# Diagonal taps on TensorE for a third of a long depthwise convolution, and GpSimd's products moved to VectorE

## The chip, the cores and the metric

The kernel runs on one core of one Trainium2 chip. A core has five engines that run side by side, each with an instruction queue of its own: TensorE (matrix products), VectorE, ScalarE and GpSimd (elementwise work), and SyncE, which here issues the weight loads. The engines wait for each other by counting semaphores. The metric is the device time of one execution, in microseconds (us); lower is better. The time before is 1533.48 us, the median of three runs (1533.14 to 1535.83).

## The reference, cut to what matters

Two transformer blocks run one after the other on 256 tokens of 1024 channels. The first one (attention and a feed-forward part) and the last part of the second (a feed-forward part with 16,384 experts) are not touched. The second block puts 16 meta tokens ahead and projects all 272 tokens to five parts: `z`, `xbc`, `dt` and the two halves `a` and `g` of a convolution branch. Two branches follow, and one output projection of both:

```python
def causal_depthwise_conv(x, w, b):          # every channel with its own taps
    y = lax.conv_general_dilated(x, w[:, None, :], window_strides=(1,), padding=[(k - 1, 0)],
                                 feature_group_count=x.shape[-1], ...)
    return y + b

def conformer_conv(u, conv_w, conv_b, ln_g, ln_b):      # conv_w: 31 taps x 1024 channels
    a, g = jnp.split(u, 2, axis=-1)
    h = causal_depthwise_conv(a * jax.nn.sigmoid(g), conv_w, conv_b)
    mu, var = mean(h), mean(square(h - mu))
    return jax.nn.silu((h - mu) * lax.rsqrt(var + EPS) * ln_g + ln_b)

def ssd_mixer(z, xbc, dt_raw, ...):
    xbc = jax.nn.silu(causal_depthwise_conv(xbc, conv_w, conv_b))    # 4 taps x 2048 channels
    xs, bm, cm = jnp.split(xbc, ...)
    dt = jax.nn.softplus(dt_raw + dt_bias)
    y = ssd_chunked(xs, dt, -exp(a_log), bm, cm)       # chunks of 128 tokens
    y = (y + d_skip * xs) * jax.nn.silu(z)
    return y * lax.rsqrt(mean over groups(y * y) + EPS) * norm_w
```

The long convolution is 31 taps on 1024 channels. With channels on the 128 partitions these are 8 channel tiles of 256 tokens, 8 x 31 = 248 products of a tile with one tap per channel.

## The kernel before, in words

**Weights.** All weights come as 423 units of 128x1024 float32. SyncE loads them into a ring of four (`raw`). ScalarE rounds a unit to its high half (`hi_to`, L825), VectorE subtracts to get the low half (`lo_to`, L1217), both into a ring of three (`W`). TensorE takes 24 matmuls per unit (L275 to L277): high by high, high by low, low by high. So a unit can be split only when the unit three before it is used up, and ScalarE's and VectorE's steps for later units stand in their queues between their other work. `hi_to(n)` and `lo_to(n)` mean "make all units below n".

**Order.** Every engine's program is written out by hand, with no scheduler. The part of the second block at issue runs so:

1. 16 GLU units (`U_GLU`). Even units give `g` (ScalarE's sigmoid, L1023), odd ones `a`; VectorE multiplies (L1391) into the tile `GP[j]`, which has 30 zero columns ahead of it. ScalarE makes the first of 31 products of a tile with the bias (`conv_first`, L1012).
2. 16 XB units (`U_XB`), 2048 channels of `xbc`. ScalarE copies them (L1030) and makes the first of the four short taps (L1034), VectorE the three others (L1406).
3. Eight z units (`U_Z`), between which stand: the `dt` product on TensorE (L549), softplus on ScalarE and VectorE (L1419 to L1425), the cumulative sums (L555 to L557), transposes of `xs` and `bm` (L568, L578), the products with `dt` (`XDT`, L1434), the state products (L595). After ScalarE's last short-convolution work come eight Silu (L1038).
4. The layer norm: TensorE adds up the eight tiles of `CV` over the channels (L604, waits for all 31 taps of each), VectorE subtracts the mean (L1453), ScalarE squares, TensorE sums again (L283), root, reciprocal, gains, Silu.
5. The core phase: eight steps `core_a(n)`, `core_b(n)` of the chunked scan with eight units of the output projection (`conformer_units`) between them.

**The long taps.** VectorE does the other 240 products (`long_convs`, L1379): `CV[j] = GP[j] shifted * tap + CV[j]`, two tiles by turns, 30 taps each. They are dealt out as filler: five after each GLU unit from the fifth on, four after each XB unit, 15 in each `z_step`, and the rest (26) behind the last `z_step`. Queues are in order, so what stands behind a group of fillers waits for them.

**GpSimd** does twelve products of this block: two 128x2048 products `DTU` (L1741), two 1024-wide `XDE` (L1748), and eight 128x512 products of `CM` (L1755) in the core phase.

## Time and profile before

| | us |
|---|---|
| median of three runs | 1533.48 |
| the profiled execution | 1532.85 |
| its span, first to last instruction | 1531.0 |
| TensorE busy | 1417.4 (93%) |
| VectorE busy | 1095.0 (72%) |
| ScalarE busy | 700.1 (46%) |
| GpSimd busy | 24.7 (2%) |
| L1379, the long taps, x240 | 101.4 |
| L1217, the low halves, x423 | 518.3 |

The page also cuts the span in 40 slices of 38.3 us and gives the busy share of each in tenths; granted clock 10 is full speed, 2.4 GHz.

```profile
PE   6999699998998548889999999999999999999997
...
DVE  4555466544899995665799997788879888655554
```

PE is TensorE, DVE VectorE, ACT ScalarE, POOL GpSimd. VectorE is at nine tenths or more in the slices 12 to 15, 421 to 574 us, and TensorE is at its lowest in two of these.

### The profile page before, as it was taken

The numbers are of one execution on the slowest core, as the hardware profiler recorded it, in microseconds if no ns is written. First come the engines' busy times: TensorE is split into PE (matmuls) and PEld (weight loads), VectorE is DVE, ScalarE is ACT, GpSimd is POOL, SyncE is SP. The second block draws the span as 40 slices with busy tenths as digits, with TensorE's granted clock in tenths as the row PEclk, the third lists the DMA queues.
The fourth block names the chain that finished last, engine by engine and source line by source line (L and its number), as shares of the span: only waits on it lengthen the run. The fifth ranks groups of instructions, "written<-read, shape, count | busy, mean of one in ns | idle before, by whom it ended". The sixth has DMA issues, their size and how long they took to land.

```text
span 1531.0 us, 25947 instructions
## 1 busy us (share of the span) xinstructions
PE 1417.4 (93%) x10882; PEld 1294.0 (85%) x10882; DVE 1095.0 (72%) x1773; ACT 700.1 (46%) x939; POOL 24.7 (2%) x20
## 2 busy tenths in 40 slices
PE   6999699998998548889999999999999999999997
PEld 5877599997988547789999999999998888888886
DVE  4555466544899995665799997788879888655554
ACT  4554355443554416545544445333343343444443
POOL 0000000000000201100000000000000000000000
PEclk9999799999999679989999999999999999999999
DMA  6433155664444212246566556555555555566663
GB/s 230 113 97 97 42 173 185 194 196 135 126 150 138 69 42 70 62 123 176 153 190 187 185 180 187 158 158 160 153 160 157 165 156 162 172 187 191 198 188 110
DMA packets 63621, 228.64 MB, mean 149 GB/s; under 512 B 7313, under 2 KB 8209, under 8 KB 63377
## 3 DMA queue, kind: packets, MB, share of 16 engines
q1 hardware_dynamic: 61776, 223.90, 48.7%
q10 hardware_dynamic: 1728, 3.09, 0.5%
q8 instruction: 86, 1.41, 0.4%
q14 instruction: 31, 0.25, 0.0%
HBM read 225.91 MB, written 1.05 MB: 148 GB/s over the span
## 4 chain that ended last, share of the span: by engine, by line
PE 79%; DVE 16%; ACT 3%; issue 1%; DMA 1%; ACTq 0%; DVEq 0%
PE ps L275 15%; PE ps L276 15%; PE ps L277 15%; PE ps L779 8%; PE ps L781 8%; PE ps L780 8%; DVE plain L1379 6%; DVE W L1217 4%; PE ps L748 3%; PE ps L283 2%; DVE plain L1406 1%; DVE RSI L1223 1%; DVE plain L1230 1%; ACT W L825 1%; PE ps L435 1%
## 5 line engine op out<-in xcount | busy, mean ns | idle before, releaser
L1217 DVE TENSOR_TENSOR W<-raw,W 128x1024 fp32r<-128x1024 f32 x423 | 518.3, 1230 | 263.9 <-ACT W L825 263.7
L825 ACT ACTIVATE W<-raw 128x1024 fp32r<-128x1024 f32 x423 | 446.3, 1057 | 390.5 <-PE ps L781 216.1
L275 PE MATMUL ps<-XH,W 128*128 128x256 f32 (+1 forms) x1784 | 513.1, 288 | 17.6 <-DVE W L1217 15.3
L276 PE MATMUL ps<-XL,W 128*128 128x256 f32 (+1 forms) x1784 | 508.8, 285 | 0.0
L277 PE MATMUL ps<-XH,W 128*128 128x256 f32 (+1 forms) x1784 | 505.8, 284 | 0.0
L275 PEld LDWEIGHTS ps<-XH,W 128*128 128x128 f32 x1784 | 339.9, 191 | 20.3 <-issue 17.2
L277 PEld LDWEIGHTS ps<-XH,W 128*128 128x128 f32 x1784 | 341.8, 192 | 0.0
L276 PEld LDWEIGHTS ps<-XL,W 128*128 128x128 f32 x1784 | 340.3, 191 | 0.1
L779 PE MATMUL ps<-W,HH 128*128 128x512 f32 x512 | 205.6, 402 | 0.8 <-ACT hid L1182 0.8
L781 PE MATMUL ps<-W,HL 128*128 128x512 f32 x512 | 202.9, 396 | 0.0
L780 PE MATMUL ps<-W,HH 128*128 128x512 f32 x512 | 202.9, 396 | 0.0
L781 PEld LDWEIGHTS ps<-W,HL 128*128 128x128 f32 x512 | 96.4, 188 | 23.4
L779 PEld LDWEIGHTS ps<-W,HH 128*128 128x128 f32 x512 | 96.4, 188 | 23.1 <-issue 1.0
L780 PEld LDWEIGHTS ps<-W,HH 128*128 128x128 f32 x512 | 96.6, 189 | 22.0
L1379 DVE SCALAR_TENSOR_TENSOR plain<-plain,vec 128x256 f32<-128x256 f32 x240 | 101.4, 496 | 0.0
L1182 ACT ACTIVATE hid<-ps 128x512 f32<-128x512 f32 x64 | 38.3, 599 | 118.8 <-PE ps L277 118.7
L276 PE MATMUL ps<-F1L,W 128*128 128x256 f32 x256 | 70.7, 276 | 0.0
L275 PE MATMUL ps<-F1H,W 128*128 128x256 f32 x256 | 70.7, 276 | 0.0
L277 PE MATMUL ps<-F1H,W 128*128 128x256 f32 x256 | 70.7, 276 | 0.0
L1648 DVE TENSOR_TENSOR onehot<-onehot,RSI 128x1536 bf16<-128x1536 bf16 x64 | 61.0, 953 | 0.0
L1644 DVE TENSOR_TENSOR onehot<-RSI 128x1024 bf16<-128x1024 bf16 x64 | 44.3, 692 | 22.2 <-PE ps L748 21.5
L748 PEld LDWEIGHTS ps<-onehot 128*128 128x128 bf16 x1536 | 50.0, 97 | 10.3 <-issue 8.8
(268 smaller groups left out, 1630.6 us busy)
## 6 DMA issues: line engine op xcount, KB each, us to landing
raw<-in_w_dn SPq DMA_DIRECT2D x128, 512.0 KB, 3.7
raw<-in_w_up SPq DMA_DIRECT2D x128, 512.0 KB, 3.6
raw<-in_w_ff SPq DMA_DIRECT2D x64, 512.0 KB, 4.1
raw<-in_w_in SPq DMA_DIRECT2D x57, 512.0 KB, 3.7
raw<-in_w_out SPq DMA_DIRECT2D x24, 512.0 KB, 3.7
raw<-in_w_q SPq DMA_DIRECT2D x16, 512.0 KB, 3.7
raw<-in_w_kv SPq DMA_DIRECT2D x4, 512.0 KB, 3.7
plain1a<-in_memT ACTq DMA_DIRECT2D x1, 1024.0 KB, 11.0
```

The source lines that it names most:

```text
L275: e.matmul(out, wh, xh, start=first, stop=False, skip_group_check=shared)
L276: e.matmul(out, wh, xl, start=False, stop=False, skip_group_check=shared)
L277: return e.matmul(out, wl, xh, start=False, stop=last, skip_group_check=shared)
L748: t = e.matmul(ps[b][:, r * 64:r * 64 + 64], OA[:, r // 2, :, r % 2], OB[:, r // 2, j, :, r % 2], start=j == 0, stop=j == 2)
L779: e.matmul(ps[b][:, :], HH[:, c % 8, tok], wh, start=c == 0, stop=False)
L780: e.matmul(ps[b][:, :], HH[:, c % 8, tok], wl, start=False, stop=False)
L781: return e.matmul(ps[b][:, :], HL[:, c % 8, tok], wh, start=False, stop=c == 127)
L825: e.activation(W[:, u % NSLOT, 0, :], raw[:, u % NRAW, :], ACT.Copy).then_inc(s["hi"], 1)
L1217: e.tensor_tensor(W[:, u % NSLOT, 1, :], raw[:, u % NRAW, :], W[:, u % NSLOT, 0, :], ALU.subtract).then_inc(s["lo"], 1)
L1379: e.scalar_tensor_tensor(CV[:, j, :], GP[:, j, 16 + k:272 + k], V("ccw", 31 * j + k), CV[:, j, :], ALU.mult, ALU.add).then_inc(cv[j], 1)
L1644: e.tensor_tensor(OA, pairs(IOTA, 128), at(0, 128), ALU.is_equal).then_inc(s["oa"], 1)
L1648: e.tensor_tensor(OB.rearrange("p t q a b -> p (t q) a b"), EB.rearrange("p (t q a) -> p t q a", t=4, q=1) .broadcast_to([128, 4, 3, 128]) ...
```

## The change

78 of the 248 products go to TensorE: taps 0 to 7 of the tiles 4 and 5, and all 31 of the tiles 6 and 7. For each, ScalarE writes a 128x128 matrix with the tap's 128 channel values on its diagonal (`diagonals`, the identity times a column), into a ring of 64 that lies where the output halves `YCH`, `YCL` will be written later. TensorE multiplies it with the shifted tile and adds up in PSUM bank 7 (tiles 4, 5) and 0 (tiles 6, 7). ScalarE copies the sum with the bias to `CV` (`conv_out`). VectorE keeps 166 products: tiles 0 to 3 from tap 1 on, 4 and 5 from tap 8 on. Its fillers are four per GLU unit, two per XB unit, 14 per `z_step`, two left at the end. The z units use PSUM banks 5 and 6 only. GpSimd's twelve products of this block are done by VectorE, each at a written place.

```diff
+CONV_AT = {3: (0, 1), 7: (2, 3)}
+PE_TAPS = [(j, k) for j, n in ((4, 8), (5, 8), (6, 31), (7, 31)) for k in range(n)]
+NDIAG = 64
...
-        z_bank = (5, 6, 7, 0)
+        z_bank = (5, 6, 5, 6)
...
+            def conv_taps():
+                for p, (j, k) in enumerate(PE_TAPS):
+                    if k == 0:
+                        e.wait_ge(s["xb"], 12 if j < 6 else 13)
+                        e.wait_ge(s["gp"], j + 1)
+                        e.wait_ge(s["pads"], 2)
+                    e.wait_ge(s["diag"], p + 1)
+                    e.matmul(ps[7 if j < 6 else 0][:, half(j)], DIAG[:, p % NDIAG, :], GP[:, j, 16 + k:272 + k],
+                             start=k == 0, stop=...).then_inc(s["cp"], 1)
+                    yield
...
             t.then_inc(s["dt_mm"], 1)
+            tap(8)
             next(z)
+            tap(8)
             e.wait_ge(s["dt_v"], 3)
...
             next(z)
+            tap(8)
...
+                    else:            # after the second transpose group of each chunk
+                        tap(8)
...
+            tap(8)
             next(z)
+            tap(len(PE_TAPS))
...
             def conformer_units():
-                e.wait_ge(s["z_out"], 4)
+                e.wait_ge(cv[6], 31)
+                e.wait_ge(cv[7], 31)
...
+            def diagonals():
+                e.wait_ge(s["unit"], U_GLU)
+                for p, (j, k) in enumerate(PE_TAPS):
+                    if p >= NDIAG:
+                        e.wait_ge(s["cp"], p - NDIAG + 1)
+                    e.activation(DIAG[:, p % NDIAG, :], ident, ACT.Copy,
+                                 scale=V("ccw", 31 * j + k)).then_inc(s["diag"], 1)
+                    yield
+            def conv_out(j, n):
+                e.wait_ge(s["cp"], max(p for p, (i, _) in enumerate(PE_TAPS) if i // 2 == j // 2) + 1)
+                e.activation(CV[:, j, :], ps[7 if j < 6 else 0][:, j % 2 * 256:j % 2 * 256 + 256], ACT.Identity,
+                             bias=V("ccb", j)).then_inc(cv[j], n)
...
+                for _ in range(2):   # once behind each of the 32 GLU and XB units
+                    next(diags)
...
             next(z)
+            conv_out(4, 8)
+            conv_out(5, 8)
+            for _ in diags:
+                pass
...
             next(z)
+            conv_out(6, 31)
+            conv_out(7, 31)
...
-                for tiles in ((0, 1), (2, 3), (4, 5), (6, 7)):
-                    for k in range(1, 31):
+                for tiles, first in (((0, 1), 1), ((2, 3), 1), ((4, 5), 8)):
+                    for k in range(first, 31):
...
-                    for _ in range(5):
+                    for _ in range(4):
...
-                for _ in range(4):
+                for _ in range(2):
...
-                for _ in range(15):
+                for _ in range(14):
```

The three kinds of GpSimd products (`DTU`, `XDE`, `CM`) are taken out of its program and put into VectorE's, with the same operands: `DTU` before the second `z_step`, `XDE` after each chunk's second `XDT`, `CM` right after each product of `LT` in the core phase.

VectorE between the `dt` step and the second chunk's transposed products. Before (L1379 the taps, L1422 and L1425 the `dt` step, L1217 the low halves, L1434 `XDT`):

```order
283 L1379 SCALAR_TENSOR_TENSOR plain<-plain,vec 128x256 x15
284 L1422 SCALAR_TENSOR_TENSOR small<-small 128x48
285 L1425 SCALAR_TENSOR_TENSOR small<-small 128x48
286 L1217 TENSOR_TENSOR W<-raw,W 128x1024
287 L1379 SCALAR_TENSOR_TENSOR plain<-plain,vec 128x256 x15
288 L1434 TENSOR_TENSOR plain<-ps,small 16x512
289 L1217 TENSOR_TENSOR W<-raw,W 128x1024
290 L1379 SCALAR_TENSOR_TENSOR plain<-plain,vec 128x256 x15
291 L1434 TENSOR_TENSOR plain<-ps,small 16x512
292 L1434 TENSOR_TENSOR plain<-ps,small 128x512
```

And of the changed kernel (L1446 the taps, L1489 and L1492 the `dt` step, L1284 the low halves, L1497 `DTU`, L1507 `XDT`, L1514 `XDE`):

```order
283 L1446 SCALAR_TENSOR_TENSOR plain<-plain,vec 128x256 x14
284 L1489 SCALAR_TENSOR_TENSOR small<-small 128x48
285 L1492 SCALAR_TENSOR_TENSOR small<-small 128x48
286 L1284 TENSOR_TENSOR W<-raw,W 128x1024
287 L1497 TENSOR_TENSOR plain<-cstb,small 128x2048 x2
288 L1446 SCALAR_TENSOR_TENSOR plain<-plain,vec 128x256 x14
289 L1507 TENSOR_TENSOR plain<-ps,small 16x512
290 L1284 TENSOR_TENSOR W<-raw,W 128x1024
291 L1446 SCALAR_TENSOR_TENSOR plain<-plain,vec 128x256 x14
292 L1507 TENSOR_TENSOR plain<-ps,small 16x512
293 L1514 TENSOR_TENSOR plain<-plain,small 16x1024
294 L1507 TENSOR_TENSOR plain<-ps,small 128x512
```

The two `DTU` products stand ahead of 14 taps, and the `XDE` product of the first chunk ahead of the second chunk's first `XDT`.

TensorE at the end of the stretch. Before, from the last state products (L595) on, the two z matmuls that follow standing for a whole unit:

```order
3203 L568 MATMUL ps<-cst,plain 128x128 x4
3204 L595 MATMUL ps<-plain 128x256 x8
3205 L275 MATMUL ps<-XH,W 128x256
3206 L276 MATMUL ps<-XL,W 128x256
...
3228 L277 MATMUL ps<-XH,W 128x256
3229 L604 MATMUL ps<-plain,cst 128x256 x8
```

And of the changed kernel (L564 the taps, L629 the state products, L640 the channel sums):

```order
3208 L600 MATMUL ps<-cst,plain 128x128 x4
3209 L564 MATMUL ps<-plain,diag 128x256 x8
3210 L629 MATMUL ps<-plain 128x256 x8
3211 L564 MATMUL ps<-plain,diag 128x256 x8
3212 L283 MATMUL ps<-XH,W 128x256
3213 L284 MATMUL ps<-XL,W 128x256
...
3236 L564 MATMUL ps<-plain,diag 128x256 x22
3237 L640 MATMUL ps<-plain,cst 128x256 x8
```

Eight taps stand on either side of the state products, and 22 directly ahead of the channel sums.

## Rows read from the trace of the kernel before

**Rows 1.** busy time by stage, with (instructions); granted clock, DMA share, GB/s

```profile
core 0: us, PE busy (x) PEld busy (x) DVE busy (x) ACT busy (x) POOL busy (x), PEclk, DMA share, GB/s
403.00:440.00 37.00, 36.78 (x293) 36.50 (x292) 37.00 (x75) 16.04 (x23) 0.00 (x0) 1.00 0.53 157
440.00:480.00 40.00, 33.11 (x257) 32.16 (x256) 40.00 (x82) 21.45 (x34) 0.00 (x0) 1.00 0.48 144
513.00:574.00 61.00, 30.83 (x185) 27.86 (x185) 56.99 (x116) 12.87 (x18) 11.50 (x4) 0.72 0.15 43
595.00:652.00 57.00, 51.48 (x382) 39.87 (x380) 37.77 (x56) 30.48 (x46) 10.28 (x8) 1.00 0.26 75
```

**Rows 2.** VectorE in order of time: start, us, instruction, [idle before <-releaser]

```profile
441.44 1.23 DVE L1217 TENSOR_TENSOR W<-raw,W 128x1024 fp32r<-128x1024 f32 x1
...
504.75 0.22 DVE L1419 TENSOR_TENSOR small<-ps,vec 128x48 f32<-128x48 f32 x1
...
506.08 6.02 DVE L1379 SCALAR_TENSOR_TENSOR plain<-plain,vec 128x256 f32<-128x256 f32 x15
...
512.26 0.21 DVE L1425 SCALAR_TENSOR_TENSOR small<-small 128x48 f32<-128x48 f32 x1
514.99 2.25 DVE L1217 TENSOR_TENSOR W<-raw,W 128x1024 fp32r<-128x1024 f32 x1 [2.52 <-ACT W L825]
517.16 9.38 DVE L1379 SCALAR_TENSOR_TENSOR plain<-plain,vec 128x256 f32<-128x256 f32 x15
...
557.69 16.31 DVE L1379 SCALAR_TENSOR_TENSOR plain<-plain,vec 128x256 f32<-128x256 f32 x41
575.78 2.74 DVE L1453 SCALAR_TENSOR_TENSOR plain<-ps,plain 128x256 f32<-128x256 f32 x8 [1.77 <-PE ps L604]
```

**Rows 3.** the chain that ended last, in order of time: start, us, what

```profile
573.66 2.08 PE ps L604 x4
579.21 3.47 PE ps L283 x16
```

**Rows 4.** VectorE by line and shape, whole span: busy us, mean ns, idle before

```profile
L1586 DVE TENSOR_TENSOR hid<-hid,cst 128x2048 f32<-128x2048 f32 x4 | 9.0, 2285 | 0.0
```

**Rows 5.** GpSimd in order of time, columns as in group 2

```profile
512.54 8.16 POOL L1741 TENSOR_TENSOR plain<-cstb,small 128x2048 f32<-128x2048 f32 x2 [145.08 <-DVE small L1425]
...
544.47 1.90 POOL L1748 TENSOR_TENSOR plain<-plain,small 128x1024 f32<-128x1024 f32 x1 [7.71 <-DVE plain L1434]
```

**Rows 6.** ScalarE in order of time, columns as in group 2

```profile
499.45 4.51 ACT L1038 ACTIVATE plain<-plain 128x544 f32<-128x544 f32 x8
503.87 1.04 ACT L825 ACTIVATE W<-raw 128x1024 fp32r<-128x1024 f32 x1
...
509.76 0.22 ACT L1058 ACTIVATE small<-vec 128x16 f32<-128x16 f32 x1
```

**Rows 7.** ScalarE by line and shape, 380 to 600 us

```profile
L1012 ACT ACTIVATE plain<-plain,vec 128x256 f32<-128x256 f32 x8 | 4.8, 596 | 12.6 <-DVE plain L1391 12.6
```

**Rows 8.** TensorE in order of time, columns as in group 2

```profile
436.23 0.36 PE L275 MATMUL ps<-XH,W 128*128 128x272 f32 x1 [0.22 <-DVE W L1217]
...
496.38 5.43 PE L549 MATMUL ps<-WDT,plain 128*128 128x16 f32 x48
```

**Rows 9.** TensorE by line and shape, 512 to 575 us

```profile
L568 PE MATMUL ps<-cst,plain 128*128 128x128 f32 x16 | 3.0, 316 | 9.8 <-DVE plain L1434 9.8
L595 PE MATMUL ps<-plain 128*128 128x256 f32 x8 | 2.0, 392 | 0.0
```

**Rows 10.** VectorE in the core phase, columns as in group 2

```profile
618.01 0.69 DVE L1472 TENSOR_TENSOR plain<-plain,ps 128x512 f32<-128x512 f32 x1 [1.22 <-ACT plain L1097]
619.44 1.46 DVE L1217 TENSOR_TENSOR W<-raw,W 128x1024 fp32r<-128x1024 f32 x1 [0.74 <-ACT W L825]
```

**Rows 11.** two short stretches, columns as in group 1

```profile
528.00:536.00 8.00, 1.35 (x7) 1.15 (x7) 6.80 (x17) 1.53 (x2) 1.12 (x1) 0.50 0.25 66
544.00:552.00 8.00, 7.55 (x49) 6.69 (x49) 7.25 (x15) 2.14 (x3) 1.90 (x1) 1.00 0.19 66
```

More of the change, by code:

```diff
@@ L149, in build @@
             (8, 272), (8, 272), (8, 272), (8, 302), (8, 256), (16, 275), (16, 272), (8, 256), (8, 256), (2, 272)])
-        YCH, YCL = (tensor(P2, n, [128, 16, 256], F32R) for n in ("YCH", "YCL"))
+        P2a = stack()
+        YCH, YCL = (tensor(P2a, n, [128, 16, 256], F32R) for n in ("YCH", "YCL"))
+        P2a.close()
+        P2b = stack()
+        DIAG = tensor(P2b, "diag", [128, NDIAG, 128])
+        P2b.close()
         DTU = [plain2[:, at:at + 2048].rearrange("p (a b) -> p a b", b=128) for at in (8 * 272, 16 * 272)]
@@ L539, in z_units, with tap @@
                 for m in range(8):
-                    if m % 2 == 0:
-                        e.wait_ge(s["xb"], (10, 11, 12, 13)[m // 2])
+                    if m < 4:
+                        if m % 2 == 0:
+                            e.wait_ge(s["xb"], 10 + m // 2)
+                    elif m % 2 == 0:
+                        e.wait_ge(s["z_out"], m // 2 - 1)
                     h_unit(U_Z + m, ps[z_bank[m // 2]][:, half(m)], slice(16, 272))
                     yield
+            def conv_taps():
[6 more added lines that the diff above has]
+                    e.matmul(ps[7 if j < 6 else 0][:, half(j)], DIAG[:, p % NDIAG, :], GP[:, j, 16 + k:272 + k],
+                             start=k == 0, stop=p + 1 == len(PE_TAPS) or PE_TAPS[p + 1][0] != j).then_inc(s["cp"], 1)
+                    yield
+            taps = conv_taps()
+            def tap(n):
+                for _ in range(n):
+                    next(taps, None)
             z = z_units()
@@ L659, in core_b @@
                     e.wait_ge(s["st_v"], 4)
+                    e.wait_ge(cv[4], 8)
+                    e.wait_ge(cv[5], 8)
                 for r in range(4):
@@ L1013, in conv_first @@
                              scale=V("ccw", 31 * j)).then_inc(cv[j], 1)
+            def diagonals():
[6 more added lines that the diff above has]
+                    yield
+            diags = diagonals()
+            def conv_out(j, n):
+                e.wait_ge(s["cp"], max(p for p, (i, _) in enumerate(PE_TAPS) if i // 2 == j // 2) + 1)
+                e.activation(CV[:, j, :], ps[7 if j < 6 else 0][:, j % 2 * 256:j % 2 * 256 + 256], ACT.Identity,
+                             bias=V("ccb", j)).then_inc(cv[j], n)
             for m in range(16):
@@ L1035, in scalar_program @@
                                      scale=V("scw", 4 * i)).then_inc(s["xi"], 1)
+                for _ in range(2):
+                    next(diags)
             for i in range(0, 16, 2):
@@ L1407, in vector_program @@
                                                    ALU.mult, ALU.add).then_inc(s["xc"], 1)
-                for _ in range(4):
+                for _ in range(2):
                     next(convs, None)
@@ L1426, in vector_program @@
                                    ALU.mult).then_inc(s["dt_v"], 1)
+            lo_to(U_Z + 1 + 3)
+            e.wait_ge(s["dt_v"], 3)
+            for c in range(2):
+                e.tensor_tensor(DTU[c], upper.rearrange("p (a b) -> p a b", a=1).broadcast_to([128, 16, 128]),
+                                DTA[:, 1 + c, :].rearrange("p (a b) -> p a b", b=1)
+                                .broadcast_to([128, 16, 128]), ALU.mult).then_inc(s["du"], 1)
             z_step(1)
@@ L1437, in vector_program @@
                         z_step(2 + c)
+                if c < 2:
+                    e.wait_ge(s["xdt"], 2 * c + 2)
+                    e.wait_ge(s["dc_a"], 2)
+                    e.tensor_tensor(per_head(XDE[c][0:n, :]), per_head(XDT[c][0:n, :]),
+                                    spread(DC[0:n, c * 16:c * 16 + 16], n, 16), ALU.mult).then_inc(s["xde"], 1)
             for hf in range(2):
@@ L1474, in vector_program @@
                                     ALU.mult).then_inc(s["ltm"], 1)
+                    g, c = divmod(n, 2)
+                    e.wait_ge(s["cm"], n + 1)
+                    e.tensor_tensor(q4(CM[:, n % 2, :]), q4(CM[:, n % 2, :]),
+                                    XO[:, 12 + g, 16 + 128 * c:144 + 128 * c].rearrange("p (a b) -> p a b", a=1)
+                                    .broadcast_to([128, 4, 128]), ALU.mult).then_inc(s["cmm"], 1)
                 if n in (0, 1, 2, 4, 5, 6, 8, 9):
@@ L1737, in gpsimd_program @@
             e.memset(XB[:, :, 0:3], 0.0).then_inc(s["pads"], 1)
-            e.wait_ge(s["dt_v"], 3)
-            e.wait_ge(s["dt_mm"], 1)
-            for c in range(2):
-                e.tensor_tensor(DTU[c], upper.rearrange("p (a b) -> p a b", a=1).broadcast_to([128, 16, 128]),
-                                DTA[:, 1 + c, :].rearrange("p (a b) -> p a b", b=1)
-                                .broadcast_to([128, 16, 128]), ALU.mult).then_inc(s["du"], 1)
-            for c in range(2):
-                n = chunk[c][1]
-                e.wait_ge(s["xdt"], 2 * c + 2)
-                e.wait_ge(s["dc_a"], 2)
-                e.tensor_tensor(per_head(XDE[c][0:n, :]), per_head(XDT[c][0:n, :]),
-                                spread(DC[0:n, c * 16:c * 16 + 16], n, 16), ALU.mult).then_inc(s["xde"], 1)
-            for n in range(8):
-                g, c = divmod(n, 2)
-                e.wait_ge(s["cm"], n + 1)
-                e.tensor_tensor(q4(CM[:, n % 2, :]), q4(CM[:, n % 2, :]),
-                                XO[:, 12 + g, 16 + 128 * c:144 + 128 * c].rearrange("p (a b) -> p a b", a=1)
-                                .broadcast_to([128, 4, 128]), ALU.mult).then_inc(s["cmm"], 1)
         block = ctx.enter_context(nc.Block())
```

3 lines of the change are left out of this document (1 added, 2 removed).

## The prediction

> **What bounds the kernel now.** I read the stages first: how busy each engine is between two times. Up to 440 us TensorE and VectorE are both full. From 440 to 574 us VectorE alone is full, 40.0 of 40.0 and 57.0 of 61.0 us, while TensorE falls to half busy and to a mean granted clock of 0.72 [rows 1]. Then VectorE in order of time: its tap products L1379 run back to back, and behind the sixth weight split stand 41 of them in one block, up to 573.9 us; the mean subtraction L1453 starts at 575.78 [rows 2]. The chain that ended last runs through that block, then through the last two channel sums of L604 [rows 3]. So the end of this stretch is VectorE's number of products. The 51.5 busy us of 57 on TensorE in the core phase [rows 1] say that this phase belongs to TensorE.
>
> **What goes from VectorE, and what comes.** A product costs 6.02/15, less the overlap of one, so 0.396 us [rows 2]. VectorE loses 14 products of tiles 4 and 5 and 60 of tiles 6 and 7: 74 x 0.396 = 29.3 us. It gains two 128x2048 products before the channel sums; the same shape in another stage takes 2.285 us [rows 4], 2.2 paced, so 4.4 us. And two 1024-wide ones at the price of a weight split, 1.14 (506.08 less 504.75, less 0.19 for L1419) [rows 2], 2.3 us. Part of that was already paid: GpSimd's 8.16 us [rows 5] lie over a split of 2.25 us and 15 products of 9.38 us, where 1.14 and 5.94 are usual [rows 2]: 4.5 us lost by VectorE. So moving these two costs nothing net, and VectorE's own balance is -29.3 - 0.1 + 2.3 = about -27 us.
>
> The Trainium skill says in "SBUF — State Buffer", section "Who interferes with whom", that GpSimd and a VectorE operation with two SBUF inputs take an exclusive lock on a shared port pair, for whole instructions. The rows above agree as to direction; by a full exclusion the old place would have cost 8.2 us and not 4.5, the move would gain 3.7 us more, and since the second XDT (below) hangs on it, the time would be 1519.8.
>
> **What comes onto TensorE.** 78 products of a 128x128 float32 diagonal with 256 float32 columns. The shape stands in L283: 16 records are 8 products in 3.47 us, 0.434 each, at full clock; at half clock L604 shows 2.08 us for two [rows 3]. 78 x 0.434 = 33.9 us. I take that; the other end is 78 x 1.04 = 81 us. **Onto ScalarE** come 78 diagonals of 128x128 with a scale column, less four first taps. Between 0.22 us (128x16) [rows 6] and 0.60 us (128x256 with a column each of scale and bias) [rows 7]; I take 0.35, so 27 us, of which 64 lie in the two projection loops, where a pair of units leaves ScalarE 2 us free and more.
>
> **Walking it through.** "Unit" is a weight unit: 24 matmuls, 37.0/293 x 24 = 3.0 us on TensorE [rows 1].
> - GLU units: both engines were full [rows 1]. VectorE loses two products, 0.8 us, per pair of units, and falls below TensorE's 6.0. TensorE ran at its own pace already, so it ends about where it did, 436.0 us, 0.2 before the first XB unit [rows 8].
> - XB units: VectorE's pair is (504.75 - 441.44)/8 = 7.91 [rows 2], now less four products, 6.33; TensorE 6.0. The first pair waits some 1.5 us for ScalarE's first-tap operation, then VectorE is 0.3 us per pair slower than TensorE. The 16 units took 496.38 - 436.23 = 60.2 us [rows 8] and now 49.5: TensorE is through at 485.5, VectorE at 491 instead of 504.7.
> - Hand-over, with less cover than before. ScalarE has to finish eight Silu (4.5 us) before it makes the high half of the third z unit; that one ended at 504.9 [rows 6], 8.5 us behind the last XB unit (496.4 [rows 8]). With two diagonals more: 485.5 + 8.5 + 0.7 = 494.7. VectorE waits there for some 3.5 us; it did not wait before. Behind that wait stand its tap products and the step L1425, at 501.9 instead of 512.3 (split 1.14, 14 products 5.5, two small ones). Then ScalarE's next high half, which stands behind the sums of TensorE, lets VectorE wait: 2.5 us in the trace [rows 2], now 3.6, since TensorE first finishes eight of its taps. The next split ends at 506.6, the two 2048-wide products at 511.0, 14 products at 516.5, the first XDT at 517.2, split and 14 products more, the second XDT at 524.5.
> - TensorE meanwhile: dt product 5.1 us (with half clock behind it, as its 5.43 us of 16-column matmuls do no dense work [rows 8]), 8 taps, a unit, 8 taps, the cumulative sums from 502.9, a unit, 8 taps, a unit, 8 taps; at 518.3 it waits for the second XDT until 524.5. From there on it has its own work to do: five groups of transposes (0.6 each), three units (9.0), 46 taps (20.0), four state products (4.0) [rows 9], eight channel sums (3.5): 39.5 us, and 2.1 us for one unit at half clock behind the 6 us idle. That is 566.1.
> - VectorE has its last product done at 555.7. So **TensorE becomes the bound**: the block of 22 taps behind the last-but-two z unit, then two ScalarE copies that lie beside the first six channel sums.
> - The channel sums ended at 575.74 and end at 566.1: 9.6 us. Behind them the norm is the same chain; the next z unit runs at full clock instead of partly at half, 0.3 us. ScalarE's load of the root table, which lay beside the 41 products, now follows the two copies directly, up to 0.6 us against.
> - Core phase: VectorE takes eight 128x512 products of 0.6 us. They go into the waits for ScalarE's split, 0.74 us behind an L1472 of 0.69 [rows 10], and TensorE does not wait for them. Zero, within 1 us either way. If the cover fails, 8 x 0.6 = 4.9 us. Everything later is untouched.
>
> Sum: 9.6 + 0.3 = 9.9 us, call it 10. The profiled execution took 1532.85 us for a span of 1531.0; that gives 1522.9. The median of the runs is 0.6 us above it, so **1523.5 us**. With the cheap ends (diagonals 0.22, no half clock behind the wait) it is 13 us less than before, with the dear ones (diagonals 0.60, each hand-over 1 us later, half clock on some eight taps and a unit more) 4 us less: 1520 to 1529.
>
> **Rivals.**
> - *TensorE stays at 1.2 GHz through the taps: slower.* The clock is at 0.50 in the stretch 528 to 536 us, where TensorE worked 1.35 us of 8, and it stays at 0.72 on the mean of the whole stage; against it, 544 to 552 us, with transposes and float32 products in it, has 1.00 at 7.55 busy us of 8 [rows 1, 11]. If the 35.5 us of matmuls behind the second XDT all ran at half clock the sums would end near 600, 24 us later than now: 1557.8. It turns slower than before from 9.7 us of additional half-clock work on, a fourth of what lies there. The Trainium skill, "TensorE: Matmul & The Clock Gate", section "Loop structure matters more than you think", warns that long waits between groups of matmuls make them run cold; I expect one such wait of 6 us, for the second XDT, where the stage had several.
> - *The taps are hidden, VectorE still bounds.* If TensorE does not wait for XDT, or its taps cost 0.25 us, the end is VectorE's, 555.7 plus 2 for the last sums: 18 us gained, 1515.5. For it: TensorE was idle for half of 513 to 574 us [rows 1]. Against: L283's 0.434.
> - *The hand-overs eat it.* Four engines now pass diagonals, taps, XDT and halves round in strict order. There are eight places in which VectorE waits for a transpose or a high half that now stands behind eight taps (3.5 us) or diagonals. At 0.8 us each over what I have, 6.4 us are lost and 3.5 gained: 1530.0. For it: VectorE waited only 2.5 us for ScalarE with more cover [rows 2]. Against: most of these waits are on an engine that isn't the bound.
> - *The change doesn't take the products away* is excluded: the order of VectorE shows 166 where 240 were.
>
> **Chances and range.** A measurement of this kernel tells 0.2%, 3 us, from no change. Forecast 0.68; TensorE cold 0.08; hidden taps 0.10; hand-overs 0.14, half of it within 0.2%. So faster 0.86, same 0.06, slower 0.08. The range takes the forecast's own ends, and reaches toward both rivals of the same sign: 1515 to 1531.
>
> **What will show it.** VectorE's last tap product near 556 and TensorE's last channel sum near 566, with a block of 22 taps right before; if VectorE's is the later, the second rival. A tap pair of records at 0.43 us; at 0.87 or more the first. Granted clock of 485 to 566 us above 0.85. An idle stretch of TensorE of about 6 us before the transposes of the second chunk. L1425's successor at 501.9. GpSimd empty after its memsets. From the mean subtraction on, all times shifted by one amount; if the core phase is longer or shorter by over 1 us, that step is wrong.

## The result, and the profile after

The changed kernel takes **1525.8 us** (median of five runs, 1521.76 to 1526.07); the kernel before, beside it on the same chip, 1533.49 (five runs, 1533.14 to 1535.83). The ratio is 0.994, with a 95% interval of 0.9926 to 0.9955. The forecast was 1523.5, with a range of 1515 to 1531. The profiled execution of after took 1521.76 us for a span of 1520.0, and is the fastest of the five by 3.5 us; the one of before took 1532.85.

Busy time of after by stage, in the columns of [rows 1]; the last row is the short stretch behind TensorE's wait for the second `XDT`:

```profile
403.00:440.00 37.00, 37.00 (x297) 37.00 (x297) 34.17 (x66) 24.55 (x48) 0.00 (x0) 1.00 0.59 172
440.00:480.00 40.00, 39.43 (x308) 38.48 (x307) 37.74 (x72) 30.40 (x62) 0.00 (x0) 1.00 0.55 160
480.00:513.00 33.00, 32.91 (x223) 30.47 (x222) 26.66 (x49) 26.20 (x51) 0.00 (x0) 0.95 0.36 110
513.00:574.00 61.00, 54.66 (x312) 49.37 (x311) 46.08 (x99) 15.41 (x27) 0.00 (x0) 0.94 0.14 43
524.00:532.00 8.00, 5.40 (x26) 5.41 (x27) 7.97 (x16) 0.00 (x0) 0.00 (x0) 0.57 0.10 34
```

TensorE is full where VectorE was [rows 1], and its mean clock from 513 to 574 us is 0.94 where it was 0.72. Instead of VectorE's idle-free row there is a VectorE that waits. In order of time, columns as in group 2 (L1284 the low halves, L1446 the taps, L1492 the end of the `dt` step, L1497 `DTU`, L1507 `XDT`, L1531 the mean subtraction):

```profile
497.69 1.23 DVE L1284 TENSOR_TENSOR W<-raw,W 128x1024 fp32r<-128x1024 f32 x1 [3.44 <-ACT W L864]
...
504.61 0.21 DVE L1492 SCALAR_TENSOR_TENSOR small<-small 128x48 f32<-128x48 f32 x1
507.50 1.23 DVE L1284 TENSOR_TENSOR W<-raw,W 128x1024 fp32r<-128x1024 f32 x1 [2.69 <-ACT W L864]
508.65 4.49 DVE L1497 TENSOR_TENSOR plain<-cstb,small 128x2048 f32<-128x2048 f32 x2
513.05 5.63 DVE L1446 SCALAR_TENSOR_TENSOR plain<-plain,vec 128x256 f32<-128x256 f32 x14
...
525.87 0.67 DVE L1507 TENSOR_TENSOR plain<-ps,small 16x512 f32<-16x512 f32 x1
...
550.84 6.42 DVE L1446 SCALAR_TENSOR_TENSOR plain<-plain,vec 128x256 f32<-128x256 f32 x16
567.10 2.74 DVE L1531 SCALAR_TENSOR_TENSOR plain<-ps,plain 128x256 f32<-128x256 f32 x8 [9.85 <-PE ps L640]
```

The 41 products ahead of the mean subtraction [rows 2] are 16, and VectorE then waits 9.85 us for TensorE. TensorE in the same stretch (L578 the `dt` product, L564 the new taps, L600 transposes of `xs`, L640 the channel sums):

```profile
488.58 5.43 PE L578 MATMUL ps<-WDT,plain 128*128 128x16 f32 x48
493.86 5.39 PE L564 MATMUL ps<-plain,diag 128*128 128x256 f32 x16
501.93 3.62 PE L564 MATMUL ps<-plain,diag 128*128 128x256 f32 x16
...
526.60 1.12 PE L600 MATMUL ps<-cst,plain 128*128 128x128 f32 x4 [6.34 <-DVE plain L1507]
...
553.94 9.67 PE L564 MATMUL ps<-plain,diag 128*128 128x256 f32 x44
563.44 3.62 PE L640 MATMUL ps<-plain,cst 128*128 128x256 f32 x16
```

16 records are eight taps. At full clock they take 3.62 us; those behind the `dt` product, partly at half clock, 5.39. On the whole page the chain that ended last has moved the same way (before it was PE 79%, DVE 16%):

```profile
PE 88%; DVE 7%; ACT 3%; issue 1%; DMA 1%; ACTq 0%; DVEq 0%
```

### How the runs are compared

Kernels of this study differ by a few us, and executions of one kernel differ by as much. So the tables use a length inside the profile, too: the **stage** from VectorE's reciprocal of the norm ahead of the projection to the reciprocal of the long convolution's norm. Of after, these two are at 384.49 and at

```profile
573.90 1.75 DVE L1290 RECIPROCAL RSI<-RSI 128x256 f32<-128x256 f32 x1 [2.93 <-ACT RSI L877]
```

and of before at 381.88 and 583.21. The stage took 201.33 us and takes 189.41, so it is 11.9 us shorter.

Two half-clock stretches stand in nearly every such stage, one some 4 us behind its start and one behind the `dt` product. Each lasts 3.4 or 6.8 us, and this varies between executions of the same kernel. "Short" below means that both last 3.4 us, "long" that both last 6.8. A third one, behind TensorE's wait for the second `XDT`, is not counted in these words: it comes and goes with that wait (6.8 us in both profiles of after, 3.4 with `DTU` back on GpSimd, none with the early `XDT`).

### The profile page after: what moved, and what is told of

It reads as the page before. It is cut to its first block, busy times and chain, and to the rows that moved or that the text cites. A ratio compares the mean times of both kernels' runs of the same rounds, so it can differ in the third digit from the quotient of the medians.

```text
span 1520.0 us, 26271 instructions
## 1 busy us (share of the span) xinstructions
PE 1444.5 (95%) x11038; PEld 1317.7 (87%) x11038; DVE 1070.7 (70%) x1711; ACT 722.5 (48%) x1017; POOL 2.5 (0%) x8
## 4 chain that ended last, share of the span: by engine, by line
PE 88%; DVE 7%; ACT 3%; issue 1%; DMA 1%; ACTq 0%; DVEq 0%
PE ps L283 17%; PE ps L284 17%; PE ps L285 17%; PE ps L818 8%; PE ps L820 8%; PE ps L819 8%; PE ps L787 3%; PE ps L564 2%; PE ps L291 2%; DVE W L1284 2%; DVE RSI L1290 1%; DVE plain L1297 1%; DVE plain L1446 1%; ACT W L864 1%; PE ps L443 1%
## 5 line engine op out<-in xcount | busy, mean ns | idle before, releaser
L1284 DVE TENSOR_TENSOR W<-raw,W 128x1024 fp32r<-128x1024 f32 x423 | 514.8, 1222 | 266.7 <-ACT W L864 266.1
L283 PE MATMUL ps<-XH,W 128*128 128x256 f32 (+1 forms) x1784 | 509.8, 286 | 9.3 <-DVE W L1284 5.2
L283 PEld LDWEIGHTS ps<-XH,W 128*128 128x128 f32 x1784 | 336.7, 189 | 11.5 <-issue 7.0
L283 PE MATMUL ps<-F1H,W 128*128 128x256 f32 x256 | 70.7, 276 | 0.0
L1446 DVE SCALAR_TENSOR_TENSOR plain<-plain,vec 128x256 f32<-128x256 f32 x166 | 68.5, 475 | 0.0
```

Of the source, the lines that this page charges most:

```text
L283: e.matmul(out, wh, xh, start=first, stop=False, skip_group_check=shared)
L1284: e.tensor_tensor(W[:, u % NSLOT, 1, :], raw[:, u % NRAW, :], W[:, u % NSLOT, 0, :], ALU.subtract).then_inc(s["lo"], 1)
L1446: e.scalar_tensor_tensor(CV[:, j, :], GP[:, j, 16 + k:272 + k], V("ccw", 31 * j + k), CV[:, j, :], ALU.mult, ALU.add).then_inc(cv[j], 1)
```

## The experiments

Each label ran beside the kernel before; ratios are given with their 95% interval. The stage and its clock are those of the one profiled execution.

| kernel | median us (runs) | ratio | stage, us | clock |
|---|---|---|---|---|
| before | 1533.49 (5) | | 201.33 | short |
| after | 1525.8 (5) | 0.994 [0.9926, 0.9955] | 189.41 | short |
| after again | 1522.79 (6) | 0.992 [0.9908, 0.9932] | 193.03 | long |
| GpSimd back | 1521.51 (4) | 0.9915 [0.9899, 0.9932] | 190.43 | long |
| only GpSimd's products moved | 1535.4 (10) | 1.0 [0.9986, 1.0014] | 204.05 | long |
| 70 taps | 1521.33 (4) | 0.9915 [0.9883, 0.9947] | 189.64 | long |
| high half early | 1523.82 (4) | 0.9937 [0.9922, 0.9953] | 189.41 | short |
| 22 products omitted | 1516.23 (4) | 0.9878 [0.9864, 0.9893] | 184.90 | long |
| taps between `dt` groups | 1521.37 (5) | 0.9915 [0.9903, 0.9928] | 189.69 | first long, second gone |
| `DTU` back | 1521.72 (4) | 0.991 [0.9889, 0.9932] | 190.39 | long |
| early `XDT` | 1514.74 (4) | 0.9887 [0.9859, 0.9914] | 183.01 | short |
| early `XDT` again | 1516.63 (4) | 0.9875 [0.986, 0.9891] | 186.45 | long |
| early, mixed, `DTU` back | 1516.01 (6) | 0.9879 [0.9859, 0.9899] | 182.86 | first short, second gone |
| combined | 1516.37 (4) | 0.9876 [0.9856, 0.9897] | 187.57 | first long, second gone |

### How far runs of one kernel differ: after again

No edit.

> The changed kernel once more, unchanged, beside the others on one chip. Its five runs lay at 1521.8 once and at 1525.2 to 1526.1 four times, and the profiled one was the 1521.8. Theory A (the runs differ by how long TensorE stays at half clock behind its idle or thin stretches, here behind the dt product: 3.4 us in the profiled run, 6.8 us in two other kernels with the same code there, 1.7 us of delay each): runs at two or more levels some 2 to 4 us apart, median 1521 to 1526, and a trace with a longer or shorter half-clock stretch between 500 and 512 us. Theory B (drift of the chip): one level, shifted with the kernel before.

The stage is 3.62 us longer than in the first profile, with the same instructions. The windows 384:396 and 486:500 us, first of after and then of this run, columns as in group 1:

```profile
384.00:396.00 12.00, 7.67 (x46) 7.06 (x47) 9.37 (x16) 7.72 (x16) 0.00 (x0) 0.86 0.08 16
486.00:500.00 14.00, 14.00 (x94) 13.07 (x94) 10.39 (x21) 12.81 (x23) 0.00 (x0) 0.88 0.41 114
```

```profile
384.00:396.00 12.00, 9.76 (x49) 8.96 (x50) 8.94 (x17) 7.94 (x16) 0.00 (x0) 0.72 0.15 45
486.00:500.00 14.00, 14.00 (x82) 12.87 (x81) 10.38 (x21) 12.82 (x22) 0.00 (x0) 0.76 0.35 110
```

Twice the clock is low for 3.4 us more: 0.86 against 0.72 of 12 us, 0.88 against 0.76 of 14 us. In the second of these windows TensorE is never idle, and does 82 matmuls where it did 94. The second pair of profiles (early `XDT`, below) differs in the same two places, by 186.45 - 183.01 = 3.44 us: 1.7 us for each. From here on a stage is compared with one of the same clock. The runs lie between 1520.9 and 1526.0 us here and between 1521.8 and 1526.1 in the first set. Theory A fits that spread, but that each run's time is set by the length of these stretches is not shown, since only one run of each set has a profile.

### What gave the 11.9 us: GpSimd's products moved alone

The kernel before with its twelve GpSimd products at the places that they have after the change, and no tap on TensorE.

```diff
+            lo_to(U_Z + 1 + 3)
+            e.wait_ge(s["dt_v"], 3)
+            for c in range(2):
+                e.tensor_tensor(DTU[c], ...)         # VectorE, as after
...
-            for c in range(2):
-                e.tensor_tensor(DTU[c], ...)         # GpSimd
```

> The kernel before with only GpSimd's twelve products moved to VectorE at the places of the changed kernel; all 240 taps stay on VectorE, which bounds the stretch. Theory A: DTU net 0, XDE +2.3 less 0.5 of contention gone, so 1 to 2 us slower than before, 1535; core phase unchanged within 0.5 us. Theory B (full lock): 1.5 to 2 us faster than before. The core phase, if CM has no cover there, +4.9 us.

The ratio is 1.0, within 0.14% or 2.1 us either way, and both theories of the expectation (1 to 2 us slower, 1.5 to 2 us faster) lie within that. The trace is sharper. VectorE's last `dt` step and its mean subtraction, the rows of [rows 2] at 512.26 and 575.78, are here

```profile
514.80 0.21 DVE L1425 SCALAR_TENSOR_TENSOR small<-small 128x48 f32<-128x48 f32 x1
578.23 2.74 DVE L1464 SCALAR_TENSOR_TENSOR plain<-ps,plain 128x256 f32<-128x256 f32 x8 [1.77 <-PE ps L604]
```

`DTU` and `XDE` lie between the two, and the distance is 63.43 us where it was 63.52: nothing gained, nothing lost. The whole stage is 204.05 for 201.33, because of the clock at its two ends. Ahead of the `dt` step it is 1.8 us longer, with a first stretch of 6.8 us instead of 3.4. Behind the start of the mean subtraction it is 1.0 us longer, where TensorE's clock stays low for 3.5 us instead of 1.3. The stretch behind the `dt` product costs nothing in either kernel: behind it TensorE waits for VectorE, 6.25 us before and 4.67 here:

```profile
512.52 0.23 PE L555 MATMUL ps<-small,cstb 16*16 16x16 f32 x2 [6.25 <-DVE small L1425]
```

```profile
515.06 0.23 PE L555 MATMUL ps<-small,cstb 16*16 16x16 f32 x2 [4.67 <-DVE small L1425]
```

VectorE's eight `CM` products leave the core phase, from the reciprocal of the norm to the last group's, at 65.07 us, where it was 65.31.

So the gain is the taps', and the moved products have no part in it. This is also the only profile with all 240 taps on VectorE and a long clock; against after again, 193.03, it is 11.0 us longer, near the 11.9 between the two short ones.

### The taps' price: 70 instead of 78, and 22 left out

```diff
-((4, 8), (5, 8), (6, 31), (7, 31))
+((4, 4), (5, 4), (6, 31), (7, 31))      # VectorE takes the other eight
```

> The changed kernel with four instead of eight taps of the tiles 4 and 5 on TensorE (70 in all, 178 products on VectorE, whose last block is 10). Theory A (TensorE bounds the end of the stretch, VectorE was done 9.9 us before the mean subtraction): TensorE loses 8 x 0.434 = 3.5 us, VectorE gets 3.2 us more and is still earlier: 3.5 us faster than the changed kernel. Theory B (the hand-overs set it, not the amount of taps): same as the changed kernel. Theory C (VectorE bounds): 3.2 us slower.

```diff
-((4, 8), (5, 8), (6, 31), (7, 31))
+((4, 8), (5, 8), (6, 20), (7, 20))      # nobody does the other 22
```

> The changed kernel with 20 instead of 31 taps each of the tiles 6 and 7: 22 products are left out, nobody does them, so its output is another. It shows what TensorE's last block costs by itself. Theory A (TensorE bounds the end): the block of 22, 9.5 us, goes, VectorE (done 9.9 us before the mean subtraction) becomes the bound, the stretch ends 9 us earlier: 9 us faster than the changed kernel, VectorE's wait before the mean subtraction falls from 9.9 to 1 us. Theory B (amount of taps does not matter): the same time.

Against after again (193.03, same clock), eight taps less are worth 3.39 us, though VectorE has eight products more: 8 x 0.434 = 3.47. TensorE's taps are on the path, VectorE's are not. 22 taps less are worth 8.13 where they take 9.5. The end of the second shows why:

```profile
552.06 6.42 DVE L1446 SCALAR_TENSOR_TENSOR plain<-plain,vec 128x256 f32<-128x256 f32 x16
560.17 2.74 DVE L1531 SCALAR_TENSOR_TENSOR plain<-ps,plain 128x256 f32<-128x256 f32 x8 [1.69 <-PE ps L640]
```

The wait of 9.85 us is down to 1.69, about the 1.77 of [rows 2], where VectorE's own last product was what the sums waited for. VectorE has become the bound again, and it cuts the last 1.4 us. In both runs TensorE as the bound, theory A, is what came.

### The wait for the Silu: high half early

ScalarE makes the high half of the third z unit before its eight Silu instead of behind them.

```diff
+            hi_to(U_Z + 3)
             for i in range(0, 16, 2):
                 e.wait_ge(s["xc"], 3 * i + 6)
```

> The changed kernel with ScalarE's high half of the third z unit made ahead of the eight Silu instead of behind them. Theory A (VectorE waits 3.4 us for that half, but what comes next waits for TensorE's cumulative sums, which stand behind 16 taps and a unit): VectorE's wait of 3.4 us goes and reappears as a longer wait before the next split (2.7 plus 3.4 less 1); the kernel gains 0 to 1 us. Theory B (the wait is on the path): 3.4 us faster than the changed kernel.

The stage is 189.41, as in after to the hundredth. The wait of 3.44 us is gone, and its time stands further down the same queue:

```profile
502.56 0.21 DVE L1493 SCALAR_TENSOR_TENSOR small<-small 128x48 f32<-128x48 f32 x1 [1.39 <-ACT small L1120]
507.44 1.23 DVE L1285 TENSOR_TENSOR W<-raw,W 128x1024 fp32r<-128x1024 f32 x1 [4.67 <-ACT W L864]
```

The split that was at 507.50 is at 507.44. It waits for ScalarE's next high half, which stands behind TensorE's cumulative sums, and these stand behind a unit and 16 taps. So the visible wait was not on the path, as theory A had it.

### The price of the move to VectorE: GpSimd back, and DTU alone

```diff
-            for c in range(2):
-                e.tensor_tensor(DTU[c], ...)         # VectorE: DTU; and XDE, CM
...
+            for c in range(2):
+                e.tensor_tensor(DTU[c], ...)         # GpSimd, as before the change
```

> The changed kernel with GpSimd's twelve products (two 128x2048 DTU, two XDE, eight CM) given back to GpSimd; the taps stay on TensorE. Theory A (mine: the move costs VectorE nothing net, as GpSimd's 8.2 us of DTU cost VectorE 4.5 us in the old place, and CM is hidden): within 1 us of the changed kernel; the second XDT 1 us earlier at most, and the 14 taps beside DTU stretched by 4 to 5 us. Theory B (full exclusive lock): the time of both DTU, 8.2 us, is lost by VectorE before the second XDT, TensorE waits 3.7 us longer there, and the kernel is 3.7 us slower than the changed one. Theory C (the move is where part of the cost of the change lies): 2 to 5 us faster than the changed one.

The same with `DTU` alone:

> The changed kernel with only the two 128x2048 DTU products given back to GpSimd; XDE and CM stay on VectorE. From the traces of the GpSimd-back kernel (split of 4.00 us instead of 1.22 plus 4.49 of DTU) I expect the two products to cost VectorE 2.8 us on GpSimd and 4.4 on itself, since GpSimd starts them while VectorE waits for ScalarE's high half: second XDT 1.6 us earlier, kernel 1.6 us faster than the changed one at equal clock, of the 2.6 us that all twelve gave; from the split before DTU to the second XDT 16.7 us instead of 18.4. If the gain of all twelve came from XDE instead, this kernel is within 0.5 us of the changed one.

Stages 190.43 and 190.39, against 193.03: both save 2.6 us, so it is `DTU` that counts, and `XDE` and `CM` are worth nothing either way. Theory A of the first expectation, within 1 us of the changed kernel, fell, and C held; the second expected 1.6 us, and the second `XDT` came that much earlier. `DTU` alone, VectorE and then GpSimd:

```profile
509.99 3.99 DVE L1284 TENSOR_TENSOR W<-raw,W 128x1024 fp32r<-128x1024 f32 x1 [4.36 <-ACT W L864]
513.90 5.62 DVE L1446 SCALAR_TENSOR_TENSOR plain<-plain,vec 128x256 f32<-128x256 f32 x14
```

```profile
505.71 7.18 POOL L1818 TENSOR_TENSOR plain<-cstb,small 128x2048 f32<-128x2048 f32 x2 [137.23 <-DVE small L1492]
```

GpSimd works from 505.71 to 512.89, and VectorE waits until 509.99. So 2.9 us lie over VectorE's work, which is a split of 3.99 us (3.91 to its successor) instead of 1.15: 2.8 us lost, 4.4 saved, 1.6 net. The other 1.0 us comes behind it: TensorE waits 4.70 us for the second `XDT` instead of 6.36, and the half-clock stretch that follows lasts 3.4 us instead of 6.8.

### The wait for the second XDT: early XDT

Seven instead of 14 products in the z steps 1 and 2, so that VectorE reaches the first chunk's `XDT` earlier; the last block has 30 instead of 16.

```diff
-                for _ in range(14):
+                for _ in range((14, 7, 7, 14, 14, 14)[m]):
```

> The changed kernel with 7 instead of 14 filler taps in the second and third z steps of VectorE, the 14 taken out done at its end. Nothing is left out. Theory A (TensorE waits 6.3 us for the second XDT, and runs one unit at half clock behind it, on the path that sets the end): the second XDT comes 5.5 us earlier, the wait shrinks to about 1 us, the half-clock stretch goes, TensorE's last channel sum 6 to 8 us earlier, kernel 6 to 8 us faster than the changed one; VectorE's last tap stays near 557 and leaves 1 to 3 us of wait. Theory B (the wait is absorbed further on): same as the changed kernel.

> The changed kernel with seven instead of 14 products in the z steps 1 and 2, once more, beside the kernel that also takes the 128x2048 products back. Theory (half-clock stretches differ between executions of one kernel, and nothing else does): the stage is 183.0 us where the clock is low for 3.4 us three times between the norms, as in its first profile, and 1.7 us longer for each such stretch of 6.8 us; median 1513.5 to 1518 us. Rival (the first profile was a lucky one): stage above 187 us with the same clock.

The stage is 183.01 against 189.41 (both short), and 186.45 against 193.03 (both long): 6.4 and 6.6 us, in two pairs of profiles. In order of time on TensorE and by stage, of the first run:

```profile
518.84 0.66 PE L600 MATMUL ps<-cst,plain 128*128 128x128 f32 x4 [0.79 <-DVE plain L1507]
527.96 0.65 PE L600 MATMUL ps<-cst,plain 128*128 128x128 f32 x4 [1.28 <-DVE plain L1507]
...
513.00:566.00 53.00, 50.92 (x299) 45.40 (x298) 44.25 (x93) 13.81 (x21) 0.00 (x0) 1.00 0.16 50
```

The wait of 6.34 us is 0.79 and 1.28, and the clock behind it is 1.00. The medians are 1514.74 and 1516.63, against 1525.8 and 1522.79 for after. After was not run beside it, so the ratios to the kernel before are what can be compared: the second, up to 0.9891, lies clear of both of after's (from 0.9908 on), the first, up to 0.9914, touches one of them. The rival, that the first profile was a lucky one, falls with the second: 183.01 and two times 1.7 us are 186.4, and it was 186.45.

### The clock behind the dt product: taps between its groups

```diff
                                  stop=k == 7)
+                if i < 2:
+                    tap(4)
             t.then_inc(s["dt_mm"], 1)
             tap(8)
```

> The changed kernel with four of the first eight taps between the first and second, and four between the second and third group of the 16-column dt matmuls, which otherwise run 5.4 us in a row. Same work. Theory A (the half clock behind the dt product comes from that thin stretch): no half-clock stretch between 500 and 512 us, TensorE reaches the cumulative sums 2 to 3 us earlier, runs closer together, 1 to 3 us faster than the changed kernel in the median. Theory B (the clock falls there for another reason): the stretch stays, and dt is 3.5 us later with nothing gained.

The half-clock stretch is gone: TensorE's window from 488 to 513 us

```profile
488.00:513.00 25.00, 25.00 (x168) 23.16 (x167) 16.91 (x33) 18.02 (x32) 0.00 (x0) 1.00 0.27 74
```

has 1.00. The edit does more than the expectation says, though: `tap(8)` behind the `dt` product stays, so TensorE now has 24 taps ahead of the cumulative sums instead of 16, and 14 instead of 22 ahead of the channel sums.

The stage is 3.34 us shorter than after's at long clock, and that is the price of a stretch of 6.8 us at half clock, 3.4. TensorE begins the cumulative sums 124.50 us behind the stage's start, in after again 124.36: the eight additional taps, 8 x 0.434 = 3.5 us, fill the time that the half clock took, and are missing from the block of 22 at the end. The wait for the second `XDT` stays 6.36. So theory A was right about the clock and wrong about the sums. The move of the taps by itself would gain nothing, as TensorE has no idle time ahead of the sums; and where the stretch would have lasted 3.4 us, the gain should be 1.7 (an estimate from the same rows, with no pair of profiles for it). The `dt` product's result reaches VectorE 2.8 us later, which costs nothing: a wait of 3.62 us for it stands in place of the wait for the Silu, and the next split starts at 114.97 us of the stage, before at 114.94.

### Two attempts at all of it

First, both edits above with all GpSimd products back and 74 taps; the place of the extra taps as in the run before.

> All that the other runs pointed to, nothing left out: 7 instead of 14 fillers in the second and third z steps, 74 instead of 78 taps on TensorE, four taps between each two groups of the dt product, GpSimd's twelve products back on GpSimd. If the gains add (6.4 for the earlier XDT; up to 2.1 more from GpSimd, as much as TensorE still waits for XDT; 1.7 for four taps; 1.7 to 3.4 for the clock behind the dt product) and VectorE does not become the bound before: 10 to 12 us faster than the changed kernel, 1509 to 1512 us. If VectorE's queue bounds as soon as TensorE's waits are gone (its last tap was 4.3 us ahead of the mean subtraction in the kernel with the earlier XDT): 8 us faster at most, and its wait before the mean subtraction below 0.5 us.

1516.37 us: no better than early `XDT` alone. VectorE's last block has 34 products and ends at 560.66, and TensorE waits for it within the channel sums:

```profile
560.32 3.78 PE L642 MATMUL ps<-plain,cst 128*128 128x256 f32 x8 [3.90 <-DVE plain L1448]
```

Four sums at half clock, 3.78 us where they take 1.8. The expectation had VectorE's wait for the sums below 0.5 us, and it was 3.48: the step "VectorE is just in time" was missed by its lateness and by the clock that falls when TensorE waits for it. This profile is of the slowest of the four runs, 1520.55 us against 1515.3 to 1516.8 for the others, so the late end may not be theirs.

Then without the eight extra taps, with 78 taps and `DTU` alone on GpSimd.

> The changed kernel with seven instead of 14 products in the z steps 1 and 2, the two 128x2048 products back on GpSimd, and four taps each behind the first and the second of the three groups of 16-column products (the eight taps that stood behind all three; none in addition). Theory (behind the second XDT TensorE's own work sets the end): against the kernel with the seven-product steps alone, TensorE loses its remaining waits of 0.79 and 1.28 us before that XDT, and the half clock behind the dt product, 1.7 us; the other 1.65 us that VectorE is spared goes into its wait ahead of the mean subtraction, 4.3 us there. Stage from norm to norm 183.0 less 3.0, about 180 us; whole time 1511 to 1513 us. Rival (the 16-column products end later when taps stand between them, and VectorE's wait for them moves every later step): 0.9 us saved at most, stage 182 us or more.

Stage 182.86, not 180, so the theory fell. The rival had the right size, but not the right cause, since no step of VectorE moved to later. There are 16 taps ahead of the cumulative sums, as in early `XDT`, and without the half clock TensorE is through them 119.39 us behind the stage's start instead of 121.07. But then it waits 1.02 us for VectorE's `dt` step, which ends at 120.36 where it ended at 120.34. So of 1.7 us only 0.6 are left. At the second chunk's transposes TensorE waits 1.22 us where it waited 0.79. GpSimd gives VectorE nothing here: VectorE waits only 2.08 us behind the `dt` step, where it waited 2.69, so more of GpSimd's products (502.93 to 511.09) lies over its work. TensorE at the sums, then VectorE:

```profile
502.90 0.21 PE L587 MATMUL ps<-small,cstb 16*16 16x16 f32 x2 [1.02 <-DVE small L1493]
504.93 2.69 DVE L1285 TENSOR_TENSOR W<-raw,W 128x1024 fp32r<-128x1024 f32 x1 [2.08 <-ACT W L865]
507.54 6.20 DVE L1447 SCALAR_TENSOR_TENSOR plain<-plain,vec 128x256 f32<-128x256 f32 x7
```

A split of 2.69 us (2.61 to its successor) for 1.15 and seven products in 6.13 for 2.77: 4.8 us lost for 4.4 saved.

## Why the prediction was right, point by point

Times of after stand 2.6 us later than the prediction's from the start of the stage on (384.49 against 381.88, in code that the change does not touch), so 2.6 is taken off below.

- **TensorE through its XB units at 485.5, VectorE at 491.** 488.58 and 493.87, so 486.0 and 491.3.
- **Hand-over.** VectorE waits 3.44 us for the high half behind the Silu, 3.5 said; the `dt` step ends as L1492 at 504.61, so 502.0, 501.9 said. The next wait is 2.69 for 3.6: 0.9 too much, since TensorE was through the eight taps and the sums in time.
- **DTU** 4.49 us, 4.4 said. **Second XDT** ends at 526.54, so 523.9, 524.5 said; TensorE waits 6.34 for 6.2 and has half clock behind it.
- **TensorE from there to the last channel sum**: 41.6 us said, 567.06 - 526.60 = 40.5 found. VectorE's last tap ends 9.8 us earlier (557.26, so 554.7; 555.7 said). **TensorE is the bound**, as forecast; the experiments with 70 and with 56 taps show it at 0.42 and 0.37 us per tap of stage.
- **A tap** is 0.434 us at full clock, as L283 had it. A diagonal is 0.30: fourteen in 4.20 us, for 0.35.
- The channel sums end 182.57 us behind the stage's start instead of 193.86 [rows 3]: 11.3 saved, 9.6 said. These 1.7 us are the 0.6 by which the second `XDT` comes earlier, and 1.1 of TensorE's work behind it.
- From there to the reciprocal 6.84 us instead of 7.47: 0.6 saved, 0.3 said. **Core phase** 65.06 instead of 65.31: zero, as said.
- Not foreseen: 2.6 us lost ahead of the stage and 1.7 won behind the core phase (from the norm's reciprocal to the next norm's 92.96 instead of 94.67, where one half-clock stretch is missing). Both are clock stretches in unchanged code. The profiled pair is 11.9 + 1.7 - 2.6 = 11.0 us apart, the medians of the two sets 7.7 and 12.7. So there is luck in how near 1523.5 came to the median of 1525.8: the stage gained 11.9 us where 9.9 were said, and the medians of one and the same kernel are 3 us apart.

**The term that was mis-sized** is the one in "moving these two costs nothing net", with the balance of 4.4 us for VectorE against 4.5 lost under GpSimd. It is true of the kernel before, as the run with the products moved alone shows (63.43 us for 63.52). It is not of the changed kernel: there GpSimd would start its 7.2 us while VectorE waits for ScalarE, so only 2.9 us would collide. The prediction had that wait in its own walk-through (3.6 us), one line behind the step, and priced the move by the old place. Cost: 1.6 us, with the clock behind it 2.6, which the smaller terms above more than made up.

What it said of full exclusion was wrong too. It set GpSimd's whole 8.16 us against the 4.5 lost, and took the difference as a sign against exclusion. But VectorE waited until 514.99 [rows 2], so only 5.7 us of GpSimd's work [rows 5] lay over VectorE's. The first instructions in that stretch, one by one:

```profile
512.54 3.61 POOL L1741 TENSOR_TENSOR plain<-cstb,small 128x2048 f32<-128x2048 f32 x1 [145.08 <-DVE small L1425]
514.99 2.25 DVE L1217 TENSOR_TENSOR W<-raw,W 128x1024 fp32r<-128x1024 f32 x1 [2.52 <-ACT W L825]
516.11 4.59 POOL L1741 TENSOR_TENSOR plain<-cstb,small 128x2048 f32<-128x2048 f32 x1
517.16 3.83 DVE L1379 SCALAR_TENSOR_TENSOR plain<-plain,vec 128x256 f32<-128x256 f32 x1
```

The split begins within GpSimd's first product and ends 1.1 us behind it, which is about its own time. GpSimd's second product takes 1.0 us more than its first, and the split is still at work in that time. The first tap ends 0.3 us behind the second product, and the taps behind it take 0.48 us each. So the engines take turns, instruction by instruction. VectorE's loss and GpSimd's together are 4.5 + 1.0 of 5.7 us of overlap here, 2.8 + 0 of 2.9 with `DTU` back, and 4.8 + 1.0 of 6.2 in the last run: nearly all of it. The Trainium skill, "SBUF — State Buffer", section "Who interferes with whom", calls it an exclusive lock, and these rows agree. What it costs is the overlap, not GpSimd's duration.

**The rivals.** TensorE cold: the clock was 0.94 from 513 to 574 us, and a tap's pair of records 0.43. Hidden taps: VectorE's last tap is 9.8 us ahead of the last sum. Hand-overs: VectorE's waits behind the second `XDT` are 0.28, 0.45 and 1.28 us, and none of them is on the path. The Trainium skill's warning, in "TensorE: Matmul & The Clock Gate", section "Loop structure matters more than you think", that long waits between matmuls make them run cold, held for one wait (6.34 us, then a clock of 0.57 for 8 us) and not for waits of 1.3 us and less (1.00 throughout, early `XDT`).

**Left open.** Why the half-clock stretches last 3.4 or 6.8 us in different executions was not tried. Nor was any other split of the products between the z steps than 14 and 7, so early `XDT` is not shown to be the best there is; nor do the runs tell it from the last two kernels, with medians of 1516.37 and 1516.01.

## What to carry to other kernels

When work goes from the engine that bounds a stage to another, walk the stage once more with the new owner as the bound: here the largest thing left was one wait of 6.3 us of the new bound, put there by filler work of the old one, and moving 14 filler products behind it was worth 6.5 us, half as much as the whole change. Price GpSimd's work beside VectorE by the stretch in which both would be working at its new place, not by its duration or by what it cost at the old place. Price a half-clock stretch only where its engine does not wait for another one right behind it. Where kernels are 3 us apart, compare stages of equal clock, and take a second profile of the same kernel before believing either.

## What the runs showed that was not expected

- The half-clock stretches behind a thin stretch of TensorE work last 3.4 or 6.8 us in different executions of the same kernel, and the longer ones cost 1.7 us more where TensorE is the bound: two of them made 3.62 us between two profiles of after, and 3.44 between two of early `XDT`.
- Behind 5.4 us of 16-column matmuls the clock falls though TensorE's records show it 100% busy (14.00 of 14.00 us from 486 to 500 us, clock 0.88). With eight taps between the three groups it stayed at 1.00. Where TensorE waits for VectorE right behind such a stretch, as in the kernel before, the stretch costs nothing.
- GpSimd's two 2048-wide products take 8.16 us where VectorE works beside them for some 6 us and 7.18 where it does so for 2.9: GpSimd gives up about 1 us, VectorE 4.5 to 4.8, and together that is nearly all of the overlap.
